# Two attentions: turns and products dealt out at every second score chunk, turns ahead of products

## What is computed

```
# differential attention, 4 heads, two score maps a head
s1 = q1 @ k1.T * scale + bias          # bias: ALiBi and the chunk mask
s2 = q2 @ k2.T * scale + bias
a  = softmax(s1) - lam * softmax(s2)
o  = a @ v
...
# latent attention, 4 heads, one score map a head, 128 + 64 columns of q and k
s = (q @ k.T) * scale + mask
o = softmax(s) @ v
```

## Time and profile before

| | us |
|---|---|
| timed runs | 2750.43 (median), 2747.48, 2755.34 |
| the profiled execution | 2756.73 |
| its span, first to last instruction | 2754.9 |
| PE busy in the span | 2609.4 (95%) |
| DVE, ACT, POOL busy | 1624.1 (59%), 1217.6 (44%), 326.9 (12%) |
| mean granted clock of TensorE | 0.975 of full speed |
| differential attention, first score to last product | 499 to 878 |
| latent attention, the same | 884 to 1238 |

### The profile page before, as it was taken

How to read it: one execution, slowest core, us unless ns; L and a number is a source line. 1 busy time by engine, 2 the same in 40 slices (tenths; PEclk the granted TensorE clock), 3 DMA queues, 4 the chain that set the end, 5 groups by cost and what they waited for, 6 DMA issues and landing times. The chain is left out here.

```text
span 2754.9 us, 35499 instructions
## 1 busy us (share of the span) xinstructions
PE 2609.4 (95%) x12220; PEld 2143.8 (78%) x12220; DVE 1624.1 (59%) x3484; ACT 1217.6 (44%) x2182; POOL 326.9 (12%) x301
## 2 busy tenths in 40 slices
PE   8999998799998999998997999999999999999997
PEld 7996787566666888886775788878888887878786
DVE  5113303789885666654445767677667465565665
ACT  6112312467675555555444333353335344343553
POOL 1011001122211212220000000000000001111132
PEclk9999998799999999998998999999999999999999
DMA  6323417824442111006566677657746355666787
GB/s 220 124 100 101 114 62 243 215 70 104 116 139 74 40 38 43 28 13 194 161 213 221 201 230 226 208 173 224 222 122 223 111 193 126 151 172 150 180 175 131
DMA packets 332475, 403.03 MB, mean 146 GB/s; under 512 B 23552, under 2 KB 239856, under 8 KB 323600
## 3 DMA queue, kind: packets, MB, share of 16 engines
q1 hardware_dynamic: 314736, 368.87, 42.5%
q0 software_dynamic: 17568, 31.99, 8.0%
HBM read 244.32 MB, written 156.48 MB: 145 GB/s over the span
## 5 line engine op out<-in xcount | busy, mean ns | idle before, releaser
L2782 PE MATMUL ff_ps_x<-ff_mv_hi_p,ff_st_hi_p 128*128 128x512 f32 x1024 | 402.0, 393 | 20.7 <-DVE ff_mv_lo_p L2666 14.9
L2782 PE MATMUL ff_ps_x<-ff_mv_hi_p,ff_st_lo_p 128*128 128x512 f32 x1024 | 401.4, 392 | 0.0
L2782 PE MATMUL ff_ps_x<-ff_mv_lo_p,ff_st_hi_p 128*128 128x512 f32 x1024 | 401.3, 392 | 0.0
L2661 DVE TENSOR_TENSOR ff_st_lo_p<-ff_ps_sum_p,ff_st_hi_p 128x512 fp32r<-128x512 f32 x256 | 176.4, 690 | 193.3 <-ACT ff_st_hi_p L2539 192.7
L2782 PEld LDWEIGHTS ff_ps_x<-ff_mv_hi_p,ff_st_hi_p 128*128 128x128 f32 x1024 | 193.8, 189 | 64.2 <-issue 23.7
L2782 PEld LDWEIGHTS ff_ps_x<-ff_mv_hi_p,ff_st_lo_p 128*128 128x128 f32 x1024 | 193.9, 189 | 40.5
L2782 PEld LDWEIGHTS ff_ps_x<-ff_mv_lo_p,ff_st_hi_p 128*128 128x128 f32 x1024 | 193.9, 189 | 40.3
L1806 PE MATMUL ml_ps_s<-ahead_keys,ml_qs 128*128 128x416 f32 (+14 forms) x880 | 200.1, 362 | 9.2 <-DVE ml_qs L1779 6.5
L2782 PE MATMUL ff_ps_w<-ff_mv_hi_p,ff_st_hi_p 128*128 128x512 f32 x512 | 199.5, 390 | 0.1
L2782 PE MATMUL ff_ps_w<-ff_mv_lo_p,ff_st_hi_p 128*128 128x512 f32 x512 | 199.3, 389 | 0.0
L2782 PE MATMUL ff_ps_w<-ff_mv_hi_p,ff_st_lo_p 128*128 128x512 f32 x512 | 199.3, 389 | 0.0
(11 more groups left out here) (240 smaller groups left out, 5830.5 us busy)
## 6 DMA issues: line engine op xcount, KB each, us to landing
st_raw<-in_w_ff SPq DMA_DIRECT2D x64, 512.0 KB, 6.2
scr_hid<-ff_pieces SPq DMA_DIRECT2D x128, 256.0 KB, 2.7
st_raw<-scr_hid SPq DMA_DIRECT2D x64, 512.0 KB, 5.1
ring<-in_w_ff SPq DMA_DIRECT2D x28, 1024.0 KB, 7.7
scr_t<-ring SPq DMA_DIRECT2D x24, 1024.0 KB, 6.0
ring<-scr_t SPq DMA_DIRECT2D x24, 1024.0 KB, 8.7
scr_acc<-ff_pieces POOLq DMA_DIRECT2D x64, 256.0 KB, 4.0
ring<-scr_u SPq DMA_DIRECT2D x14, 1024.0 KB, 8.9
```

Source lines behind the costliest of these rows:

```text
L2661: dve.tensor_tensor(st_lo[kind][:, :, :], stationary(kind, n % 2), f32(st_hi[kind][:, :, :]), ALU.subtract).then_inc(st_lo_ready, 1)
L2782: m = pe.matmul(bank[:, :], w[kind][:, k], a[kind][:, k], start=start and k == 0 and i == 0, stop=stop and k == KH - 1 and i == 2, skip_gr ...
```

## The change

In `head_steps` of both attentions, steps are no longer dealt out after every step of the row list, but only after score chunks with an odd number (and after the last step of a phase). What is due is collected in `batch`, and `turns_first` puts the turns of a batch ahead of its products and outs. The lead steps go out as before, in their old order, but also only at those places. The counts of all instructions stay as they are.

```
+def turns_first(batch):
+
+
+    turns = [step for step in batch if step[0] == "turn"]
+    return turns + [step for step in batch if step[0] != "turn"]
...
                     last = at == len(rows_part) - 1
+                    if not last and (step[0] != "chunk" or step[2] % 2 == 0):
+                        continue
+                    batch = []
                     while lead_steps and (last or part > start * (1 - (len(lead_steps) - 1) / n_lead)):
                         steps.append(lead_steps.pop(0))
                     while body_steps and (last or part > start + (1 - start) * (1 - len(body_steps) / n_body)):
...
-                        steps.append(body_steps.pop(0))
+                        batch.append(body_steps.pop(0))
+                    steps += turns_first(batch)
                 steps += lead_steps + body_steps
```

## The result

The change makes the kernel slower: 2771.51 us, median of eight runs (2765.53 to 2775.14), against 2749.82 for eight runs of before (2746.02 to 2756.93). The ratio is 1.0074, 95% interval 1.0059 to 1.0089: 20 us (16 to 24). The forecast was 2762.0 and its range reached to 2774.0, so the sign and the range held, and the size fell short: +11.6 was forecast, +20.3 came, and +19.5 in a later comparison. The profiled execution took 2770.84, its span 2769.1.

What follows compares the result with a forecast made beforehand. PE was taken to set both attention stages, full in the latent one, with at most 12.5 us to win in three differential heads. Terms sum to +11.6 on the median 2750.4, giving 2762.0 us; range 2753 to 2774.

Steps and rivals of the forecast that it cites:

- start of a head, differential: Heads 1 to 3: ACT makes tile 1's exponential before the out and first copy, so product 0 comes later; +4.2 us.
- queries at chunk 54: Differential heads 1 and 2: group 3's queries queue behind keys that wait for product 8, now later; +0.8 us.
- gain at chunk 87: Differential attention: DVE gets chunk 57 sooner, so PE's wait for DVE at chunk 87 shrinks 0.45 a head; -1.8 us.
- out, latent: Four latent heads: the out queues behind three copies on ACT, so product 0 comes 1.43 late; +5.7 us.
- four turns in a run: Latent heads 1 to 3: four turns behind chunk 7 share three banks, turn 7 waits 0.74 a head; +2.2 us.
- rest of the latent attention: Behind latent head 3: another run of four costs 0.74, partly given back by an earlier turn 3; +0.5 us.
- the marks named in the prediction: Expected profile signs, among them product 0 waiting for ACT over 1 us and latent idle time some 6 us.
- a fall at the starts: Rival: waits at three differential head starts lower the clock, up to 3.4 us each; +22 us, 2772; 15 in 100.
- none of 1.25 did it: Argument against the clock falling: earlier waits of 1.25 us at head starts had left PE at full clock.
- runs of eight transposes at full clock: Argument that longer runs of turns would not lower the clock by themselves, in either attention; no size given.
- The delays were not taken up: Rival: query waits swallow PE's lateness in heads 1 and 2, and low parts come sooner; +6.2 us, 2757; 25 in 100.
- the faster case: Rival: DVE runs ahead, so waits for banks, turn 0 and product 0 go; -9.4 us, 2741; 8 in 100.

Runs made afterwards that it cites:

- all costs undone: Changed kernel with outs ahead of turns, queries ahead of keys, differential head starts dealt as before, latent turn 4 moved behind chunk 5: 0.9974 against the kernel before.

## Why the prediction was right in sign and short in size

By its own terms, in us a kernel; what was measured is time lost on PE in the profiles, and for the clock the share of falls by their cost.

| term | forecast | measured |
|---|---|---|
| start of a head, differential | +4.2 | +4.5 (3 x 1.50) |
| queries at chunk 54 | +0.8 | +2.3 (means of 7 and 4 profiles; overlap; 0.6 of it by product 8) |
| gain at chunk 87 | -1.8 | -1.0 (4 x 0.25) |
| out, latent | +5.7 | +5.9 (4 x 1.48) |
| four turns in a run | +2.2 | +2.5 (3 x 0.82) |
| rest of the latent attention | +0.5 | +0.7 (9.1 lost more, less 5.9 and 2.5) |
| clock at starts and at the out | 0 | +4.5 (11/24 x 3 x 1.4 + 8/20 x 4 x 1.6) |
| clock behind chunk 54 | 0 | +1.5 (2.1 a kernel against 0.6) |
| sum | +11.6 | +20.9; timed +20.3 and +19.5 |

**Right.** The three terms read as chains on ACT and DVE came out within 0.3 us each: start, out and run of four, and with the rest they make +13.6 measured against +12.6. Undoing each of them brought its waits back to those of before. Of the marks named in the prediction most appeared: product 0 and chunk 5 at the starts, ACT's exponential still 0.31 behind the reading of chunk 3 (680.31 to 680.62), both new waits in the latent attention and its 6 us of idle time. Two did not come as said: chunk 87's wait is shorter by a third and not by half, and chunk 54's is longer in head 1 alone.

**Wrong: the clock.** The prediction set a fall at the starts as a rival at 15 in 100, against it "none of 1.25 did it", and took zero in the sum. The step that failed is making one case with a yes or no of it, to come in all heads or in none. It came in two of five waits of that length, in both attentions, and cost 1.4 to 1.6 and not 3.4. As an expected number it belongs in the sum: 4.5 of the 8 to 9 us missed. The trace of before alone could not have given the number: it has no fall behind a wait of this length in the stretches of the earlier trace rows. The rival's 2772 is nearer to the measured time than the forecast's 2762, but for half by another road, and so by some luck: the latent attention, where the prediction didn't look for it, has 2.6 of the 4.5. The prediction's last line, a granted clock below 0.99 in these stretches, was the mark of its own error, and 0.98 stands in the differential one. Against the longer runs of turns the prediction set runs of eight transposes at full clock, from the earlier trace rows. Only the earlier trace rows has such a run, and the clock's row is the earlier trace rows; the argument held all the same.

**Wrong in size: chunk 54 and chunk 87.** The gain at chunk 87 was read as 0.45 a head from DVE's gap of 0.53; it is 0.25. Chunk 54 lost 2.3 instead of 0.8 in these profiles, and 1.5 more by the clock; 0.6 of that is product 8's place, the rest is transfer time that differs between executions and was read from two single waits. The timed runs show nothing of that rest: without the waits of chunk 54 the other terms make +17.1 and the change costs 19.6 there. So 20.9 against 20.3 is closer than the parts allow, and part of that is luck.

**The base.** The prediction put its differences on the median and not on the profiled execution, which stood 6.3 over it. That was sound: the second profile of before lacks the wait of 3.14 and the fall behind it.

**The other rivals.** The delays were not taken up: the waits of heads 1 and 2 did not shrink by the 1.5 that PE came later, because product 8 came later with it, and turn 7 did wait. From the bank waits only chunk 87's 1.0 came back; and the version with all costs undone and the new dealing kept is as fast as the old dealing, so the faster case had nothing to find.

The fastest kernels of the study are before with the queries issued ahead of the keys (2746.56) and the one with all costs undone (2745.50), both 0.26% below before and 1.0% below after, and not to be told apart.

## What to carry to other kernels

Where an engine that goes in order is already full, write down for each reordered batch which copy now stands ahead of the one that somebody waits for: an out that frees an accumulator goes ahead of the copies that only feed later work. Put a new wait of PE into the sum with the clock that may fall behind it, as a chance by its cost, with the chance counted over several executions: one profile shows a fall or none. Take the prices of transfers from more than one execution, since the waits for ACT and DVE repeated here to the tenth and those for the DMA did not.

## What the runs showed of the hardware

The same wait of 1.43 us on the same instruction was followed by a lower clock (0.52 for 3.4 us) in 8 heads of 20 and by none in the others, within one execution too (head 2 in after, not the other three). At 2.69 it was 4 of 4, and for 6.8 us in three of them; at another place, in head 0 of the latent attention, waits of 1.9 to 3.5 us were followed by one in 2 of 14. With the wait filled by useless matmuls of the same length the clock stayed at full in 4 heads of 4: 28 matmuls more, and a time 3.5 us lower, on intervals that overlap. The issue of one transfer of 256 KB on SP's queue, a store or a load, took 12.8 to 18.0 us when keys, bias and values had been issued just ahead, in two heads of each of fourteen profiles, and what SP issued behind it came that much later.
